# Inverting 64x64 blocks of a recurrence: the second head's solution on the other half of the partitions, and the transposed inverse turned instead of updated

## The reference, cut to what matters

```
def first_block(x, mem, ...):
    ...
        if layer % N_MIXERS == 0:
            mix, q_mem = rwkv7_time_mix(h, rw_in[j], rw_mu[j], rw_w0[j], rw_w2[j], rw_a0[j],
                                        rw_a2[j], rw_g2[j], rw_k_k[j], rw_k_a[j], rw_r_k[j],
                                        rw_lnx_g[j], rw_lnx_b[j])
```

## Time and profile before

| what | value |
|---|---|
| median of three runs | 1587.07 us (1586.98 to 1587.89) |
| the profiled execution, its own time | 1584.96 us |
| span of the profiled execution, first to last instruction | 1583.1 us |
| TensorE busy | 1518.1 us, 96% of the span |
| VectorE, ScalarE, GpSimd busy | 837.6, 544.6, 257.5 us |
| mean granted TensorE clock | 0.995 of full speed |
| the six pairs | about 91 to 414 us of the span |

### The profile page before, as it was taken

The page is one execution under the profiler, slowest core; times in us unless marked ns, Lnnn a source line. Parts: engine busy times, 40 slices in busy tenths (PEclk is TensorE's granted clock), DMA queues, the critical chain, the costliest instruction groups (busy, mean ns, idle before and its releaser), DMA issues.

```text
span 1583.1 us, 26362 instructions
## 1 busy us (share of the span) xinstructions
PE 1518.1 (96%) x11246; PEld 1204.0 (76%) x11246; DVE 837.6 (53%) x1261; ACT 544.6 (34%) x871; POOL 257.5 (16%) x183
## 2 busy tenths in 40 slices
PE   6899999998889999999999999999989999999999
PEld 4677777776668888888878886666768888888887
DVE  6555655567455445353555357668565443343343
ACT  6432333235233212121253236555434222222131
POOL 3133332321020000000010001232322220120120
PEclk9999999999999999999999999999999999999999
DMA  6220010001023323233223323322223233333323
GB/s 216 67 68 29 29 42 29 29 24 60 28 59 91 104 94 95 91 107 93 91 85 92 93 75 93 97 73 64 69 82 103 83 104 95 92 97 102 94 83 103
DMA packets 38516, 127.65 MB, mean 81 GB/s; under 512 B 4224, under 2 KB 5248, under 8 KB 38400
## 3 DMA queue, kind: packets, MB, share of 16 engines
q1 hardware_dynamic: 38400, 125.97, 25.9%
HBM read 123.86 MB, written 2.10 MB: 80 GB/s over the span
## 4 chain that ended last, share of the span: by engine, by line
PE 85%; DVE 8%; ACT 4%; issue 2%; POOL 0%; DMA 0%; SPq 0%; POOLq 0%; DVEq 0%; ACTq 0%
PE bank L915 82%; PE bank L1296 1%; PE bank L1030 1%; DVE qa L1590 1%; DVE Hlo L1488 1%; ACT Whi L1907 1%; DVE Wlo L1482 1%; DMA x<-in_xT 0%; PE bank L1099 0%; DVE qa L1588 0%; DVE ftmp L1537 0%; ACT kbr L2112 0%; ACT Hhi L1982 0%; DVE y L1758 0%; PE bank L1252 0%
## 5 line engine op out<-in xcount | busy, mean ns | idle before, releaser
L915 PE MATMUL bank<-Hhi,Whi 128*128 128x512 f32 x912 | 376.7, 413 | 18.0 <-DVE Wlo L1482 10.3
L915 PE MATMUL bank<-Hhi,Wlo 128*128 128x512 f32 x912 | 362.7, 398 | 0.0
L915 PE MATMUL bank<-Hlo,Whi 128*128 128x512 f32 x912 | 359.9, 395 | 0.0
L915 PE MATMUL bank<-Uhi,Whi 128*128 128x512 f32 x736 | 291.3, 396 | 8.9 <-DVE Ulo L1760 4.0
L915 PE MATMUL bank<-Uhi,Wlo 128*128 128x512 f32 x736 | 288.0, 391 | 0.0
L915 PE MATMUL bank<-Ulo,Whi 128*128 128x512 f32 x736 | 287.8, 391 | 0.0
L1482 DVE TENSOR_TENSOR Wlo<-Wraw,Whi 128x1024 fp32r<-128x1024 f32 (+1 forms) x177 | 226.9, 1283 | 100.1 <-ACT Whi L1907 100.0
L1907 ACT CAST Whi<-Wraw 128x1024 fp32r<-128x1024 f32 (+1 forms) x216 | 223.2, 1037 | 161.0 <-PE bank L915 147.1
L915 PEld LDWEIGHTS bank<-Hhi,Whi 128*128 128x128 f32 x912 | 172.4, 189 | 75.4 <-issue 12.6
L915 PEld LDWEIGHTS bank<-Hlo,Whi 128*128 128x128 f32 x912 | 172.1, 189 | 42.2
L915 PEld LDWEIGHTS bank<-Hhi,Wlo 128*128 128x128 f32 x912 | 172.6, 189 | 33.0
(11 more groups left out here) (297 smaller groups left out, 1722.0 us busy)
## 6 DMA issues: line engine op xcount, KB each, us to landing
Wraw<-in_wts SPq DMA_DIRECT2D x208, 512.0 KB, 3.6
bA<-in_biasA SPq DMA_DIRECT2D x12, 256.0 KB, 2.8
Wraw<-in_wts SPq DMA_DIRECT2D x8, 384.0 KB, 3.1
x<-in_xT SPq DMA_DIRECT2D x8, 256.0 KB, 4.3
X<-in_xT SPq DMA_DIRECT2D x2, 1024.0 KB, 7.2
out<-X SPq DMA_DIRECT2D x8, 256.0 KB, 2.1
bB<-in_biasB SPq DMA_DIRECT2D x4, 384.0 KB, 3.0
memX<-in_memT SPq DMA_DIRECT2D x2, 512.0 KB, 7.3
```

The lines of the kernel that those rows point to most:

```text
L915: return e.matmul(o, lhsT, rhs, start=start, stop=stop, skip_group_check=True)
```

## The change: what it does, and the diff

Head 0's items keep their place. For head 1, what the inverse is multiplied into lies on the opposite half of the partitions: T, the transposed inverse Yi, GA (both right-hand sides and the solution) are split by head, head 1's block of half g going to or coming from half 1-g. A new helper `crossed` replaces `by_tokens` for `t1`, `xu`, `gv`, and the code of `uw`; it writes head 0 to one bank and head 1 to another. `na` becomes 16 matmuls with the identity instead of 4 transposes. The updates of Yi at levels 1 to 4 (`yu`) go; in their place, behind `t1` of the next level, `xt` multiplies Xi by the identity, and ScalarE copies the result over Yi. The last level's `yu` stays as it was. Where one instruction of 512 columns on VectorE or ScalarE read one bank, two of 256 columns now read two; the first mask of Yi takes three instructions, since head 1 changes halves. Where these steps took one bank they take two. The room given to the filler is the same in sum; within a level it is 1.6 ahead of `xu` and 1.4 behind it, where it was 1.6, 0.2 and 1.2.

The core of the diff:

```diff
-        for kind in ("na", "nb", "vn", "kn"):
+        two("na", p)
+        yield 0.7
+        for kind in ("nb", "vn", "kn"):
             bank(kind, p)
             yield 0.7
...
             if l == 3:
-                bank("gv", p)
+                two("gv", p)
                 yield 0.7
-            bank("t1", p, l)
+            two("t1", p, l)
+            if l > 1:
+                two("xt", p, l - 1)
             yield 1.6
             if l < len(LEVELS) - 1:
-                bank("xu", p, l)
-                yield 0.2
-            bank("yu", p, l)
-            yield 1.2
+                two("xu", p, l)
+                yield 1.4
+        bank("yu", p)
+        yield 1.2
...
-        def by_tokens(user, lhsT, rhs):
-
-            b = bank(*user)
-            for i in range(NC):
+        def crossed(kind, key, n, lhsT, rhs, turned):
...
+            to = [bank(kind, *key, h) for h in range(2)]
+            for cp in range(4):
                 for g in range(2):
-                    x = mm(b[64 * g:64 * g + 64, 64 * i:64 * i + 64], lhsT[64 * g:64 * g + 64, i, :],
-                           rhs[64 * g:64 * g + 64, i, :], True, True)
+                    for h in range(2):
+                        here, there = g, (1 - g if h else g)
+                        if turned:
+                            here, there = there, here
+                        x = mm(to[h][64 * there:64 * there + 64, n * cp:n * cp + n],
+                               lhsT(h, 2 * cp + g, here), rhs(h, 2 * cp + g, here), True, True)
             return x
...
+        def turn_x(p, l):
+
+            w.wait_ge(S["xu_out"], 2 * N("xu", p, l))
+            crossed("xt", (p, l), 64, of_item(Xi), one(), False).then_inc(S["xt"])
...
         def level_x(p, l):
             inverse_ready(p, l)
-            by_tokens(("xu", p, l), Yi[p % 2], T1).then_inc(S["xu"])
-
-        def level_y(p, l):
-            inverse_ready(p, l)
-            by_tokens(("yu", p, l), T1, Yi[p % 2]).then_inc(S["yu"])
+            crossed("xu", (p, l), 64, of_item(Yi[p % 2]), of_item(T1), True).then_inc(S["xu"])
...
         def turn_a(p):
-            transposes(("na", p), lambda cp: AR[p % 2][:, 0, 128 * cp:128 * cp + 128]).then_inc(S["na"])
+            crossed("na", (p,), 64, lambda h, ch, half: AR[p % 2][64 * h:64 * h + 64, 0, 64 * ch:64 * ch + 64],
+                    lambda h, ch, half: c("same")[64 * h:64 * h + 64, :], False).then_inc(S["na"])
...
+            crossed("uw", (p,), 128, of_item(Yi[p % 2]), of_item(GA[p % 2]), True).then_inc(S["uw"])
...
-            for h, b in enumerate(two):
-                masked(of_head(Yi[q], h), b, 0, 128, "firstt").then_inc(S["sb_out"])
+            masked(of_head(Yi[q], 0), two[0], 0, 128, "firstt").then_inc(S["sb_out"])
+            for g in range(2):
+                here, there = (slice(64 * x, 64 * x + 64) for x in (g, 1 - g))
+                e.tensor_tensor(of_head(Yi[q], 1)[there], blocks(two[1][here, :], 128)[:, :, 0:64],
+                                bcast(c("firstt")[here], 4), ALU.mult).then_inc(S["sb_out"])
...
-            e.tensor_tensor(Xi[:], stk(MB[plan.M.at["xu", p, l]]), Xi[:], ALU.add).then_inc(S["xu_out"])
...
+            for h in range(2):
+                x = of_head(Xi, h)
+                e.tensor_tensor(x, blocks(MB[plan.M.at["xu", p, l, h]][:, 0:256], 64), x,
+                                ALU.add).then_inc(S["xu_out"])
...
+        def by_heads(kind, to, n, last=None):
+
+            def step(p, *l):
+                w.wait_ge(S[kind], N(kind, p, *l))
...
+                for h in range(2):
+                    b = MB[plan.M.at[(kind, p, *l, h)]]
+                    e.copy(of_head(to(p % 2), h)[:, :, n], blocks(b[:, 0:4 * (n.stop - n.start)],
+                                                                   n.stop - n.start)).then_inc(S[kind + "_out"])
+            return step
```

More of the change, by code:

```diff
@@ L219, in bank, with two @@
         M.give((kind, *key))
-    def two(kind, p):
+    def two(kind, *key):
         for i in range(2):
-            M.take((kind, p, i))
-        step(kind, p)
+            M.take((kind, *key, i))
+        step(kind, *key)
         for i in range(2):
-            M.give((kind, p, i))
+            M.give((kind, *key, i))
     def tile(kind, key, name, ver, ks, n=T, j0=0, keep=None, hold=None, js=None, last=True):
@@ L879, in out_of @@
         if kind in TWO:
-            p, i = user[1:]
-            return S[kind + "_out"], TWO[kind] * p + TWO[kind] - 1 + i
+            *key, i = user[1:]
+            return S[kind + "_out"], TWO[kind] * N(kind, *key) - 1 + i
         return S[kind + "_out"], N(*user)
-    TWO = {"xm": 2, "sb": 6, "sk": 4, "uw": 2, "pd": 2, "phi": 2, "yo1": 2}
+    TWO = {"xm": 2, "sb": 7, "sk": 4, "na": 2, "gv": 2, "t1": 2, "xt": 2, "xu": 2, "uw": 2, "pd": 2, "phi": 2, "yo1": 2}
     for n, s in enumerate(x for x in plan.steps if x[0] in ("rs", "hn", "kk", "tn")):
@@ L1119, in score_k, with of_item, one @@
             by_scores("sk", p, heads(kf), both(p), 128).then_inc(S["sk"])
+        def of_item(t):
+            return lambda h, ch, half: t[64 * half:64 * half + 64, 2 * (ch // 2) + h, :]
+        def one(t=c("same")):
+            return lambda h, ch, half: t[64 * half:64 * half + 64, :]
         def turn_a(p):
-            transposes(("na", p), lambda cp: AR[p % 2][:, 0, 128 * cp:128 * cp + 128]).then_inc(S["na"])
+            crossed("na", (p,), 64, lambda h, ch, half: AR[p % 2][64 * h:64 * h + 64, 0, 64 * ch:64 * ch + 64],
+                    lambda h, ch, half: c("same")[64 * h:64 * h + 64, :], False).then_inc(S["na"])
         def turn_b(p):
@@ L1146, in inverse_ready, with last_level @@
             else:
-                w.wait_ge(S["yu_out"], N("yu", p, l - 1))
-            w.wait_ge(S["t1_out"], N("t1", p, l))
+                w.wait_ge(S["xt_out"], 2 * N("xt", p, l - 1))
+            w.wait_ge(S["t1_out"], 2 * N("t1", p, l))
         def level_x(p, l):
             inverse_ready(p, l)
-            by_tokens(("xu", p, l), Yi[p % 2], T1).then_inc(S["xu"])
-        def level_y(p, l):
-            inverse_ready(p, l)
-            by_tokens(("yu", p, l), T1, Yi[p % 2]).then_inc(S["yu"])
+            crossed("xu", (p, l), 64, of_item(Yi[p % 2]), of_item(T1), True).then_inc(S["xu"])
+        def last_level(p):
+            inverse_ready(p, len(LEVELS) - 1)
+            b = bank("yu", p)
+            for i in range(NC):
+                for g in range(2):
+                    gg = slice(64 * g, 64 * g + 64)
+                    x = mm(b[gg, 64 * i:64 * i + 64], T1[gg, i, :], Yi[p % 2][gg, i, :], True, True)
+            x.then_inc(S["yu"])
         def key_values(p):
@@ L1160, in key_values @@
             w.wait_ge(S["sk_out"], 4 * p + 2)
-            by_tokens(("gv", p), AK, Vn[p % 2]).then_inc(S["gv"])
+            crossed("gv", (p,), 64, of_item(AK), of_item(Vn[p % 2]), False).then_inc(S["gv"])
         def solve(p):
[L1164 to L1172, removed]
+            w.wait_ge(S["yu_out"], p + 1)
+            w.wait_ge(S["gv_out"], 2 * p + 2)
+            w.wait_ge(S["na_out"], 2 * p + 2)
+            crossed("uw", (p,), 128, of_item(Yi[p % 2]), of_item(GA[p % 2]), True).then_inc(S["uw"])
         def increments(p):
@@ L2048, in turned @@
             return step
-        def solve(p):
-            w.wait_ge(S["uw"], p + 1)
-            for i in range(2):
-                e.copy(GA[p % 2][:, 4 * i:4 * i + 4, :], blocks(MB[plan.M.at["uw", p, i]][:], 128)).then_inc(S["uw_out"])
+        def by_heads(kind, to, n, last=None):
+            def step(p, *l):
+                w.wait_ge(S[kind], N(kind, p, *l))
+                if last and p >= 2:
+                    w.wait_ge(S[last], p - 1)
+                if p == 0 and kind == "na":
+                    mem_done(w)
+                for h in range(2):
+                    b = MB[plan.M.at[(kind, p, *l, h)]]
+                    e.copy(of_head(to(p % 2), h)[:, :, n], blocks(b[:, 0:4 * (n.stop - n.start)],
+                                                                   n.stop - n.start)).then_inc(S[kind + "_out"])
+            return step
         def outputs_within(p):
@@ L2263, in score_b @@
         def score_b(p):
-            w.wait_ge(S["sb_out"], 6 * p + 4)
+            w.wait_ge(S["sb_out"], 7 * p + 5)
             turn()
```

41 lines of the change are left out of this document (23 added, 18 removed).

## The result

The changed kernel took 1565.55 us (median of 4 executions, 1564.17 to 1573.40) against 1587.48 (4, 1586.98 to 1588.27): ratio 0.9872, 95% interval 0.9839 to 0.9904. The forecast was 1563.8 in 1550 to 1575, faster. The profiled execution took 1565.88 us, its span is 1564.0. So the gain is shown and is 1 to 1.3%; why one kernel shows 1565 and 1573 is the subject of e9.

The account below looks back on a forecast made before the run. TensorE, busy 96% of the span, was taken to set the pace. Pairs 1 to 4 gain 19.2, pair 0 3.2, pair 5 0.9: 23.3 us, from 1584.96 to 1561.7, or 1563.8 on the median's scale; range 1550 to 1575.

Parts of the forecast that it names:

- The quadrants: TensorE's small-matmul groups and `uw` on four quadrants: 0.46 us less a group, `uw` 0.9 less, 7.3 us a pair.
- The wait for `sg`: New TensorE wait before level 1's `xt`, which takes `sg`'s late-read bank: 2.1 us a pair, 2.5 in pair 0.
- `uw`'s wait: TensorE ahead of `uw`: it waits for both banks of `sb` and seven masks instead of six, 0.66 us more.
- the state step: TensorE's state step that waited 0.87 us for VectorE finds T done: 0.4 us given back a pair.
- the wait for `sb`: TensorE's wait of 1.36 us ahead of `sb`, ending a VectorE chain whose T starts earlier: 0.4 us back.
- The other waits: `xt` of level 2 waiting for a `gv` bank, and the key's spreading for the mean's readout: 0.5 us together.
- Pair 5: Last pair: savings ahead of its long chain cancel against late exponentials; only `uw`'s 0.9 us is gained, bounds -2 and 6.
- Rival C: The clock drops to 0.50 after each of five new waits, costing 2 us each: 1574; chance 0.17 together with B.
- A: Nearly all the saving lands, as waits vanish or replace others: up to 43.8 us off, 1543; chance 0.13.
- B: Readouts become the bound, `xt`'s ScalarE copies delaying `xu`: 10 us less gain, 1574; chance 0.17 together with Rival C.
- D: Slower: neighbours in `crossed` sharing a row half take turns, groups stay 0.98 us, waits remain: 1597; chance 0.06.
- E: No difference: pauses and savings cancel within 0.2%, which needs groups at just the break-even price; chance 0.02.

Follow-up runs that it names:

- e9: The changed kernel run again, unedited: median 1573.42 us over six executions, ratio 0.9905 to the kernel before.
- e1: The changed kernel with both heads on the same half, so two quadrants in place of four: 1602.35 us, ratio 1.0101 to the kernel before.
- e5: The changed kernel with the weight cast and GpSimd's subtraction Wlo issued ahead of `sq` in place of behind it: 1559.77 us, ratio 0.9829.
- e11: The kernel of e5 with 7 in place of 9 memory attention steps woven into pair 5: 1558.74 us, ratio 0.9823.
- e3: The changed kernel with the loops over couple and head swapped in `t1`, `xt`, `gv` and `na`: 1572.77 us, ratio 0.9904.
- e12: The kernel before the change, with the early cast of e5 put in: 1587.19 us against 1585.90, ratio 1.0004.
- e4: The changed kernel with the cast of Whi and GpSimd's subtraction Wlo issued behind `ta`: 1568.98 us, ratio 0.9891.
- e6: The changed kernel with `xt` of level 2 issued later, behind six large matmuls: 1571.47 us, ratio 0.9899.
- e7: The changed kernel with `uw` later, `bonus` yielding 2.6 in place of 1.0 so filler runs ahead: 1573.39 us, ratio 0.9910.

## Why the prediction was right, and where it was not

**The quadrants** were right in mechanism and size: groups of 0.51 to 0.52 where 0.50 was expected, `uw` 1.04 where 1.03 was; e1 shows that the gain is theirs alone. The 0.50 was read a little low: the row at 256.93 is reached with 26 of the 28 matmuls of `pd`, which makes 0.54 for 16.

**The wait for `sg`** was the step on which the number hung, and it stood: 2.1 forecast, 1.92 in pairs 2, 3 and 4. T started at 250.94 on VectorE and `sg` was out at 257.68, 6.7 us later, against the 6.8 from the earlier trace rows. Pair 0 waited 2.39 (2.5 forecast) behind 0.40 (0.6). Pair 1 waits 0.51 for `sg` and 1.34 ahead of a state step.

**`uw`'s wait** rose by 0.67 (0.66 forecast), the state step gave back 0.87 - 0.38 = 0.49 (0.4), the wait for `sb` 0.38 (0.4). The other waits, 0.5 in the forecast, are not there in pairs 2 and 3 (0.17 in pair 4, ahead of `C,Xi`). In their place the work shrank less than the 7.3 of the forecast, in pair 3 from 52.90 to 46.25 us of busy TensorE, 6.65; `na`, 0.62 where it was 0.43, is 0.2 of the rest. That the two cancel, and the pairs come out at 4.8 to the tenth, is luck. Pairs 1 to 4 gained 4.80, 4.78, 4.81 and 4.12 from `uw` to `uw`, forecast 4.8; the last of these lacks 0.7, with pair 5's `km,qm` and the wait of 2.25 ahead of it in it.

**Pair 5 is the term that was mis-sized**: +0.9 was forecast, -1.4 came (49.58 against 48.15). TensorE's work in it fell from 39.84 to 35.37 us, 4.5, and its idle time rose by 5.9, the exponentials first: 4.3 us of waits for L2123's slab banks, where there were 0.8. "I take these to cancel" was thus nearly right (e5, with the clock at 1.00 all through the pair, took 48.55, 0.4 more than before), and the clock took a microsecond more in the first profile. The prediction held the 1.00 behind the wait of 3.54 against a drop; behind the 2.25 ahead of `km,qm`, with 0.98 and 0.94 close before it, there was one. It is no rule either: e5 and e11 have 2.26 at the same place and the clock at 1.00 behind it.

**The sum.** The profiled execution was to fall by 23.3 us and fell by 1584.96 - 1565.88 = 19.1. The 4.2 missing are pair 5 with 2.3, the end of pair 4 with 0.7, pair 0 with 0.7 (0.3 of it a later start), and 0.4 in the tail, whose `uw` took 1.82 in place of 1.10. The change of the first medians, 21.9, hides this, since the kernel before was profiled in an execution 2.5 us under this median (2.1 under that of the first three).

**Rival C, the clock,** was priced rightly, 2 us a drop and 1574 in all, but as something that happens or not. By the prediction's own sign, a clock below 1.00 between 91 and 414 us, it was there in the first profile already, at 343 us. It happens in some executions: 6 of the 10 lie at 1570 to 1576, but only one of the first four. The chance for it was too low and its form wrong: a wait can cost its own length once more through the clock, in one execution and not in the next. That the forecast met the first median within 2 us has luck in it; e9's stands near the range's edge.

**Rivals A, B, D, E.** A falls with the wait. B: in pairs 0 to 4 no `T,Yi` waits for ScalarE's Yi, so the copies are hidden there. The Trainium skill's warning that evacuation may become the limit (TensorEngine Tiling (Array Packing), PSUM Bottleneck) holds for pair 5, where 4.3 us wait for banks that ScalarE's exponentials read. In the other pairs it holds for one bank, that of `sg` (1.92), and there it is a cast and a table load ahead of the readout that make it late. D's mechanism is refuted by the groups of 0.51 and by e3; e1, which takes the quadrants away, shows the sign that it would have had. E fell with D. ScalarE's busy time rose by 15.1 us as forecast; VectorE's fell by 10.6 us, not 15: two readouts of 256 columns are busy 0.75 us where one of 512 took 0.69, and three masks of Yi stand in the place of two. It was off the path.

## What to carry to other kernels

Small matmuls on half of the array are worth spreading over all four quadrants: it halves them, in both orders among neighbours that were tried. But read, for each step that arrives earlier, what it will find unfinished: a chain on another engine that nobody waited for (here a weight cast ahead of `sg`) becomes worth moving only then, and an edit that was worth nothing before (e12) took 6 us off the changed kernel's first median and 14 off its second (e5). Move such an instruction into idle time of its own engine, and look at who shares a memory port with what it drags along (e4). A wait moved is not a wait removed: list all readers of the late value first (e6, e7).

## What the runs showed of the hardware

- The clock after a wait does not follow from the wait alone: with 1.92 us of idle TensorE at the same place, the work behind it ran at 1.00 in one execution and at 0.50 for up to 6 us in another, at 1.3 to 2.7 us a time. Behind waits of 0.98 there it was 1.00 all nine times.
- VectorE's 0.55 us `kf` took 2.52 us while GpSimd's Wlo ran, and ended 0.28 us behind it; Wlo itself took 3.08 instead of 2.35 (e4, the same in pairs 2 to 4).
- 16 matmuls of 64x64 on four quadrants cost 0.51 us in either order of row halves (e3), on two quadrants 0.98, though there too neighbours lay on opposite row halves (the kernel before).
